# Where the ada sums are made, how rows are summed, and how wide the passes over the activations are

## The chip, the cores and the metric

The kernel runs on one core of one Trainium2 chip. Its time is the device time of one execution in microseconds (us), from the first instruction to the last; the number that counts is the median over runs. TensorE multiplies matrices, VectorE (DVE), ScalarE (ACT) and GpSimd (POOL) do the elementwise work, and SyncE (SP), ScalarE and GpSimd issue DMA transfers.

## The reference

Two blocks act on 256 tokens of width 1024, all in float32. The first has two layers, each a mixer (layer 0: pooling and a state space model; layer 1: two kinds of attention) and a gated feed-forward part, each followed by a layer norm over `ALPHA * x + h`:

```python
def swiglu(x, w_gate, w_up, w_down):
    return (jax.nn.silu(x @ w_gate) * (x @ w_up)) @ w_down      # D_FF = 2816
```

The second block takes a vector `c` and makes six rows of 1024 numbers from it, the ada rows (`m` = 0 to 5), which shift, scale and gate a short gated convolution and a squared-relu MLP:

```python
mod_lat = [m[:, None, :] for m in jnp.split(jax.nn.silu(c) @ ada_w[i] + ada_b[i], N_MOD, axis=-1)]
a_lat = modulate(rmsnorm(h_lat, g_pre), mod_lat[0], mod_lat[1])
y_lat = short_gated_conv(a_lat, sc_w_in[j], sc_conv[j], sc_w_out[j])
h_lat = h_lat + mod_lat[2] * rmsnorm(y_lat, g_post)
f_lat = squared_relu_mlp(modulate(rmsnorm(h_lat, g_pre_ff), mod_lat[3], mod_lat[4]), mlp_w_in[i], mlp_w_out[i])
h_lat = h_lat + mod_lat[5] * rmsnorm(f_lat, g_post_ff)
```

`ada_w` is 1024 x 6144, 24 MB, as much as the gate, up and down weights of 8 of the 11 feed-forward blocks.

## The kernel before

**Numbers in two parts.** Each weight chunk of 1 MB (128 partitions x 2048 float32) is loaded by SP into one of six slots, and is split there: ScalarE rounds it to fp32r (`hi`, L1136), VectorE subtracts (`lo`, L1575). Activations are split the same way into `x_hi` and `x_lo`. A product is then three fp32r passes of TensorE: hi with hi, hi with lo, lo with hi. In the projections (`col`, L565 to L567) the weight chunk's 128 columns are the stationary operand and 256 tokens stream past; in the products back to the model width (`tok3`, L572 to L574) the activations are stationary and 512 weight columns stream past. A slot is loaded again when its chunk has been used (`chunk_used`).

**A feed-forward part** (`ffn0` in layer 0, `ffn1` in layer 1) has 11 blocks of 256 hidden columns. In block i TensorE makes the gate and the up projection (a chunk each, 2 x 8 accumulation steps of three passes), into PSUM banks 4 and 5 or 6 and 7 by turns; then `rows_full` multiplies the hidden values of block i - 1 with their down chunk. ScalarE takes the silu of the gate out of PSUM (L1238), VectorE multiplies it with the up projection in PSUM (L1750, the hidden product), ScalarE and VectorE split the result (L1243, L1755). The last three down chunks (8, 9, 10) are left to the end, where each is multiplied for the first 128 tokens and then for the other 128, so that the layer norm of the first half can start early. Chunk 10 is split after block 10, with the first two chunks of the next stage: `split(first["odd"] + 1)` or `split(first["sc"] + 1)`. After that TensorE needs the normed, transposed rows before it can go on.

**The MLP** has 16 blocks of 256 hidden columns; the first three are made in halves, 13 go through `col`, relu on ScalarE (L1544) and a square on VectorE (L2112).

**The ada rows** are made during `ffn1`. GpSimd clears `modrow`, loads the bias, and loads 24 pieces of `ada_w` of 1 MB by turns into the two buffers `sq` and `r`; VectorE adds each piece, scaled by one number of silu(c) per partition, into `modrow` (`ada_step`, L423, 24 times, 2 or 3 in a block). What is left is a sum over the 128 partitions: `mod_sums` multiplies a row of `modrow` with a matrix of ones in float32 (L699), after blocks 4, 5, 7, 8 and 10, and the sixth in the convolution stage (`MOD_LAST`). ScalarE copies the sum back (`mod_copy`, L1217). When all 24 steps are done, GpSimd loads two rows of gains (`gain_row`, L482) over `sq`, and VectorE multiplies two ada rows with them (`gained`, L1723) at the end of its block 10, ahead of the split of down chunk 10 on the same queue:

```python
                    if name == "ffn1" and i == NF - 1:
                        gained(1, 0, 1.0)
                        gained(2, 1, 0.0)
```

Engines run their own queues in program order. The order of GpSimd's queue before, from layer 1's mixer on: rows of the next norm (`ln_rows("ln3")`), the clearing, the bias, the 24 pieces, a wait for all 24 steps, the two gain rows.

Of the kernel before, what the change touches and what calls it, by code (L numbers as in the profile page):

```python
# [11 lines left out]
P = 128  # L12
# [57 lines left out]
def build(nc, A, out):  # L70
    ctx = ExitStack()
    with ctx:
# [17 lines left out]
        x_hi = sb("x_hi", [P, KT, S], F32R)  # L90
        x_lo = sb("x_lo", [P, KT, S], F32R)
# [5 lines left out]
        ones = sb("ones", [P, P])  # L97
        d_skip = sb("d_skip_sb", [P, KT])
# [99 lines left out]
        def bank2(b):  # L198
            return PS[:, b, :].rearrange("p (a s) -> p a s", a=2)

# [212 lines left out]
        ADA_BLOCKS = range(1, 10)  # L413
        MOD_AT = {4: 0, 5: 1, 7: 2, 8: 3, 10: 4}
        MOD_LAST = 5
# [57 lines left out]
        def _(pool):  # L473
# [46 lines left out]

            pool.wait_ge(*sig_at("ln0", "x", 4))
            ln_rows("ln1")
            pool.wait_ge(*sig_at("ln1", "x", 4))
# [5 lines left out]
            pool.tensor_tensor(kr_cos[rr, :], kr[rr, 0, :], cos, ALU.mult).then_inc(sem("kr_cos"), 1)  # L529
            pool.wait_ge(*norm("kvn", "var", 1))  # L530
            for q in range(4):
                pool.wait_ge(sem("odd_evac"), 12 + q)
                pool.tensor_tensor(sq[rr, 2 * q:2 * q + 2, :], qm[rr, 2 * q:2 * q + 2, :],
                                   cos.rearrange("p (o s) -> p o s", o=1).to_broadcast([32, 2, S]), ALU.mult)\
                    .then_inc(sem("qm_cos"), 1)
# [3 lines left out]
                             .to_broadcast([32, MLA_H, S])).then_inc(sem("kr_rot"), 1)  # L539

            pool.wait_ge(*sig_at("ln2", "x", 4))
            ln_rows("ln3")
            pool.memset(modrow[:, :, :], 0.0).then_inc(sem("ada_zero"), 1)
            pool.wait_ge(sem("ada_zero"), 1)
            pool.dma_start(modrow[0:1, :, :].rearrange("p m d -> p (m d)"), A["ada_b_2"][0:1, :])\
                .then_inc(sem("ada_bias"), 16)
            for n in range(ADA_N):
                if n >= 2:
                    pool.wait_ge(sem("ada_fma"), n - 1)
                pool.dma_start(ada_raw[n % 2], A["ada_w_2"][0][n % KT * P:(n % KT + 1) * P, n // KT * CH:(n // KT + 1) * CH])\  # L550
                    .then_inc(sem(f"ada_landed{n % 2}"), 16)
# [8 lines left out]
        def _(pe):  # L560
# [15 lines left out]
            def col(c, bank, hi, lo, operand=None, between=None):  # L576
# [5 lines left out]
                for m in range(0, n, P):  # L582
# [3 lines left out]
                    for k in range(kt):  # L586
# [108 lines left out]
            def mod_sums(m, bank):  # L695

                pe.wait_ge(sem("ada_fma"), KT * (m // 2 + 1))
                for n in range(2):
                    last = pe.matmul(PS[:, bank + n, :], ones[:, :], modrow[:, m, n * HB:(n + 1) * HB], start=True, stop=True)  # L699
                last.then_inc(sem("mod_sum"), 1)  # L700

            def ffn(name, operand, after, src):
# [13 lines left out]
                for i in range(1, NF):  # L716
                    b = 6 - 2 * (i % 2)
                    pe.wait_ge(hid_done, o + i)
                    if name == "ffn1" and i - 1 in MOD_AT:
                        pe.wait_ge(sem("mod_row"), MOD_AT[i - 1] + 1)  # L720
                    col(at[name, "g", i], b, x_hi, x_lo)
# [3 lines left out]
                    col(at[name, "g", i] + 1, b + 1, x_hi, x_lo)  # L725
                    if name == "ffn1" and i in MOD_AT:
                        pe.wait_ge(hid_done, o + i + 1)
                        mod_sums(MOD_AT[i], 6 - 2 * ((i - 1) % 2))
# [164 lines left out]
            base = first["odd"]  # L893
            for h in range(2):
# [83 lines left out]
            def scores(a):  # L978
# [5 lines left out]
                if a == FOX_H:  # L984
                    pe.wait_ge(sem("odd_evac"), 19)
                    pe.wait_ge(sem("kr_rot"), 1)
# [54 lines left out]
            ffn("ffn1", "ln2", "pre", r_tok)  # L1041

# [20 lines left out]
            for q in range(1, 4):  # L1063
                for part in range(3):
                    col(at["sc", "c", q] + part, sc_bank(3 * q + part), x_hi, x_lo)
                    if q == 1 and part == 0:
# [4 lines left out]
                        mod_sums(MOD_LAST, 0)  # L1071
                if q == 1:
                    pe.wait_ge(sem("mod_row"), MOD_LAST + 1)
# [31 lines left out]
            for i in range(3, NM):  # L1105
                pe.wait_ge(sem("mlp_relu"), i - 3 + 4)
# [1034 lines left out]
```

## Time and profile before

| | |
|---|---|
| median of three runs | 980.95 us (979.12 to 981.13) |
| the profiled execution | 980.15 us, of which the span from first to last instruction is 978.3 us |
| TensorE busy | 944.3 us of the span, granted clock 0.997 |
| VectorE, ScalarE, GpSimd busy | 645.9, 466.6 and 62.0 us |
| weights split (L1575 on VectorE, L1136 on ScalarE) | 336.1 and 278.1 us |
| DMA | 190.5 MB, 195 GB/s in the mean |

A busy engine is not the same as one that sets the end. Matmul records overlap (each lasts longer than the distance to the next), so what a matmul costs in a dense stretch is the distance between the starts, not its duration.

### The profile page before, as it was taken

Reading aid. Unit: us, or ns where it says so; the run is one execution under the profiler, and the core shown is the slowest. Engines: PE = TensorE matmul, PEld = TensorE weight load, DVE = VectorE, ACT = ScalarE, POOL = GpSimd, SP = SyncE. Lnnn points to the kernel's source line nnn. Section 1 sums busy time; section 2 is a strip of 40 time slices with the busy share of each in tenths; the row PEclk is TensorE's granted clock in tenths of the full one; section 3 lists DMA queues with packets and bytes.
Section 4 is the critical chain, followed back from the end, with each engine's and each line's share of the span. In section 5 each row is a group of like instructions: output and inputs, shape, how many; then the busy total and the mean of one; then the engine's idle time right before and its main releaser. Section 6 shows DMA issues by size and latency. Waiting matters only on the chain.

```text
span 978.3 us, 15123 instructions
## 1 busy us (share of the span) xinstructions
PE 944.3 (97%) x6537; PEld 862.8 (88%) x6537; DVE 645.9 (66%) x737; ACT 466.6 (48%) x577; POOL 62.0 (6%) x79
## 2 busy tenths in 40 slices
PE   6999989999999999999899999999899999999997
PEld 6999879999999799876699989998799989999986
DVE  4976896645454863676659788788866865555554
ACT  6556744434343465755544343445344644444442
POOL 2034000000000000220030001000000000000000
PEclk9999999999999999999999999999999999999999
DMA  9744466565565453412579999995566456566531
GB/s 280 239 131 130 136 205 219 186 195 178 181 203 177 130 173 110 133 44 87 176 283 331 381 317 338 308 348 165 185 198 198 130 175 213 175 194 191 174 128 44
DMA packets 122282, 190.52 MB, mean 195 GB/s; under 512 B 6566, under 2 KB 103080, under 8 KB 119144
## 3 DMA queue, kind: packets, MB, share of 16 engines
q1 hardware_dynamic: 115184, 156.94, 49.5%
q0 software_dynamic: 5616, 31.78, 8.8%
q8 instruction: 52, 0.85, 0.3%
q10 hardware_dynamic: 1416, 0.83, 0.3%
q14 instruction: 14, 0.11, 0.0%
HBM read 188.49 MB, written 1.05 MB: 194 GB/s over the span
## 4 chain that ended last, share of the span: by engine, by line
PE 80%; DVE 10%; ACT 5%; issue 3%; DMA 1%; DVEq 0%; POOL 0%; ACTq 0%
PE PS L565 15%; PE PS L567 15%; PE PS L566 15%; PE PS L572 10%; PE PS L574 9%; PE PS L573 9%; DVE lo L1575 3%; ACT hi L1136 2%; PE PS L699 1%; PE PS L663 1%; DMA raw<-even_w_in 1%; DVE r L1645 1%; ACT hid L1437 1%; DMA sq<-norm_gains 1%; ACT sq L1321 1%
## 5 line engine op out<-in xcount | busy, mean ns | idle before, releaser
L1575 DVE TENSOR_TENSOR lo<-raw,hi 128x2048 fp32r<-128x2048 f32 (+2 forms) x150 | 336.1, 2258 | 168.8 <-ACT hi L1136 168.6
L565 PE MATMUL PS<-x_hi,hi 128*128 128x256 f32 x1320 | 374.4, 284 | 1.9 <-DVE x_lo L1772 1.9
L567 PE MATMUL PS<-x_hi,lo 128*128 128x256 f32 x1320 | 372.3, 282 | 0.0
L566 PE MATMUL PS<-x_lo,hi 128*128 128x256 f32 x1320 | 371.7, 282 | 0.0
L1136 ACT ACTIVATE hi<-raw 128x2048 fp32r<-128x2048 f32 (+2 forms) x150 | 278.1, 1880 | 10.2 <-DMA raw<-even_w_in 8.0
L565 PEld LDWEIGHTS PS<-x_hi,hi 128*128 128x128 f32 x1320 | 251.2, 190 | 4.3 <-DVE lo L1575 2.3
L566 PEld LDWEIGHTS PS<-x_lo,hi 128*128 128x128 f32 x1320 | 251.2, 190 | 1.9 <-issue 0.5
L567 PEld LDWEIGHTS PS<-x_hi,lo 128*128 128x128 f32 x1320 | 251.2, 190 | 0.0
L572 PE MATMUL PS<-hi,hid_hi 128*128 128x512 f32 x352 | 141.2, 401 | 1.1 <-DVE lo L1575 0.7
L574 PE MATMUL PS<-hi,hid_lo 128*128 128x512 f32 x352 | 138.6, 394 | 0.0
L573 PE MATMUL PS<-lo,hid_hi 128*128 128x512 f32 x352 | 138.5, 393 | 0.0
L572 PE MATMUL PS<-hi,x_hi 128*128 128x256 f32 (+1 forms) x256 | 81.7, 319 | 7.7 <-DVE x_lo L1674 3.5
L572 PEld LDWEIGHTS PS<-hi,hid_hi 128*128 128x128 f32 x352 | 66.1, 188 | 17.5 <-issue 3.7
L574 PEld LDWEIGHTS PS<-hi,hid_lo 128*128 128x128 f32 x352 | 66.0, 188 | 15.6
L574 PE MATMUL PS<-hi,x_lo 128*128 128x256 f32 (+1 forms) x256 | 79.8, 312 | 0.0
L573 PE MATMUL PS<-lo,x_hi 128*128 128x256 f32 (+1 forms) x256 | 79.6, 311 | 0.0
L573 PEld LDWEIGHTS PS<-lo,hid_hi 128*128 128x128 f32 x352 | 66.0, 188 | 15.1 <-issue 1.2
L1238 ACT ACTIVATE gate_s<-PS 128x512 f32<-128x512 f32 x20 | 12.0, 599 | 103.2 <-PE PS L567 103.2
L572 PEld LDWEIGHTS PS<-hi,x_hi 128*128 128x128 f32 x256 | 48.8, 191 | 13.3 <-issue 8.1
L574 PEld LDWEIGHTS PS<-hi,x_lo 128*128 128x128 f32 x256 | 48.8, 191 | 2.8
L1243 ACT ACTIVATE hid_hi<-hid 128x512 fp32r<-128x512 f32 x20 | 12.6, 632 | 80.9 <-DVE hid L1750 80.9
L573 PEld LDWEIGHTS PS<-lo,x_hi 128*128 128x128 f32 x256 | 49.0, 191 | 2.5
(280 smaller groups left out, 825.5 us busy)
## 6 DMA issues: line engine op xcount, KB each, us to landing
raw<-ffn_w_gate SPq DMA_DIRECT2D x22, 1024.0 KB, 5.4
raw<-ffn_w_up SPq DMA_DIRECT2D x22, 1024.0 KB, 5.5
raw<-ffn_w_down SPq DMA_DIRECT2D x22, 1024.0 KB, 5.0
raw<-mlp_w_in SPq DMA_DIRECT2D x16, 1024.0 KB, 5.6
raw<-mlp_w_out SPq DMA_DIRECT2D x16, 1024.0 KB, 5.0
sq<-ada_w POOLq DMA_DIRECT2D x12, 1024.0 KB, 6.3
r<-ada_w POOLq DMA_DIRECT2D x12, 1024.0 KB, 7.2
raw<-sc_w_in SPq DMA_DIRECT2D x12, 1024.0 KB, 5.3
```

Of the source, the lines that this page charges most:

```text
L565: pe.matmul(dst, wh, hi, start=start, stop=False, skip_group_check=True)
L566: pe.matmul(dst, wh, lo, start=False, stop=False, skip_group_check=True)
L567: return pe.matmul(dst, wl, hi, start=False, stop=stop_, skip_group_check=True)
L572: pe.matmul(dst, hi, wh, start=start, stop=False, skip_group_check=True)
L573: pe.matmul(dst, hi, wl, start=False, stop=False, skip_group_check=True)
L574: return pe.matmul(dst, lo, wh, start=False, stop=stop_, skip_group_check=True)
L663: last = pe.transpose(PS[:, 2 * h + n, j * P:(j + 1) * P], src[:, h, o:o + P], ident)
L699: last = pe.matmul(PS[:, bank + n, :], ones[:, :], modrow[:, m, n * HB:(n + 1) * HB], start=True, stop=True)
L1136: act.activation(split_view("hi", c), split_view("raw", c), ACT.Copy).then_inc(hi_split, 1)
L1238: act.activation(gate_s[:, i % 2, :, :], bank2(6 - 2 * (i % 2)), ACT.Silu).then_inc(silu, 1)
L1243: act.activation(hid_hi[:, i % 3, :, :], hid[:, i % 2, :, :], ACT.Copy).then_inc(hi_done, 1)
L1575: dve.tensor_tensor(split_view("lo", c), split_view("raw", c), split_view("hi", c).bitcast(F32), ALU.subtract)\
```

## The change

1. **Two thirds of the ada sums move into `ffn0`.** 16 of the 24 pieces and steps (rows 0 to 3) are done in `ffn0`, two in each of blocks 1 to 8, and 8 (rows 4 and 5) in `ffn1`, one in each of blocks 1 to 8. The rows are summed after blocks 6, 7, 9 and 10 of `ffn0` and after 9 and 10 of `ffn1`. Since the attention stage uses the memory of `modrow`, rows 0 to 3 are stored in device memory (`mods`) and loaded back at the start of `ffn1`.
2. **Row sums in two fp32r parts.** `mod_high` (ScalarE) and `mod_low` (VectorE) split a row into `mod_part`, and `mod_sums` is four fp32r matmuls. `mod_part` takes the memory of `lnrow`, the rows of the next norm, so `ln_rows("ln1")` and `ln_rows("ln3")` are now loaded after the fourth and the sixth sum. The two gain rows stand behind `ln_rows("ln3")`.
3. **512-column passes.** `x_hi` and `x_lo` become one tensor `x_both`. `wide_cols` replaces `col` in blocks 1 to 10 of both feed-forward parts and in 13 blocks of the MLP. The hi part of the weights meets both parts of x in one pass of 512 columns, the lo part meets `x_hi` in one of 256. The products hi-hi and hi-lo land side by side in PSUM, so that each chunk fills two banks (gate 4 and 5, up 6 and 7, no turns). ScalarE copies the second half out (`low_part`), VectorE adds the first; silu and relu come after the sum.

```diff
-        lnrow = sb("lnrow", [P, 2, D])
+        with ExitStack() as row_views:
+            lnrow = sb("lnrow", [P, 2, D], F32, row_views)
+        mod_part = sb("mod_part", [P, 2, D], F32R)
...
-        ADA_BLOCKS = range(1, 10)
-        MOD_AT = {4: 0, 5: 1, 7: 2, 8: 3, 10: 4}
-        MOD_LAST = 5
+        ADA_STEPS = {"ffn0": (0, 2 * KT), "ffn1": (2 * KT, ADA_N)}
+        MOD_AT = {"ffn0": {6: 0, 7: 1, 9: 2, 10: 3}, "ffn1": {9: 4, 10: 5}}
...
@@ GpSimd
             pool.wait_ge(*sig_at("ln0", "x", 4))
+            ada_loads(0, 4)
+            pool.wait_ge(sem("mod_sum"), 4)
             ln_rows("ln1")
+            pool.wait_ge(sem("mod_row"), 4)
+            pool.dma_start(mods[0:1, :], modrow[0:1, 0:4, :].rearrange("p m d -> p (m d)")).then_inc(sem("mods_moved"), 16)
...
             pool.wait_ge(*sig_at("ln2", "x", 4))
+            ada_loads(4, 6)
+            pool.wait_ge(sem("mod_sum"), 6)
             ln_rows("ln3")
...
             pool.wait_ge(sem("ada_fma"), ADA_N)
             gain_row(0)
             gain_row(1)
...
@@ TensorE
+            def wide_cols(c, bank, between=None):
+
+                pe.wait_ge(lo_split, c + 1)
+                for m in range(2):
+                    if between and m:
+                        between()
+                    cols = slice(m * P, (m + 1) * P)
+                    for k in range(KT):
+                        wh, wl = slot("hi", c)[:, k, cols], slot("lo", c)[:, k, cols]
+                        pe.matmul(PS[:, bank + m, :], wh, x_both[:, :, k, :], start=k == 0, stop=False, skip_group_check=True)
+                        last = pe.matmul(PS[:, bank + m, 0:S], wl, x_hi[:, k, :], start=False, stop=k == KT - 1,
+                                         skip_group_check=True)
+                last.then_inc(chunk_used, 1)
...
                 for n in range(2):
-                    last = pe.matmul(PS[:, bank + n, :], ones[:, :], modrow[:, m, n * HB:(n + 1) * HB], start=True, stop=True)
+                    for part in range(2):
+                        last = pe.matmul(PS[:, bank + n, :], ones_r[:, :], mod_part[:, part, n * HB:(n + 1) * HB],
+                                         start=part == 0, stop=part == 1, skip_group_check=True)
...
@@ ScalarE, block i
                     split(g + 2)
+                    split(g + 3)
+                    if i in MOD_AT[name]:
+                        mod_high(MOD_AT[name][i])
+                    n = (NF - 1) * (name == "ffn1") + i
                     act.wait_ge(chunk_used, g + 1)
                     if i >= 2:
                         act.wait_ge(hid_done, o + i)
-                    act.activation(gate_s[:, i % 2, :, :], bank2(6 - 2 * (i % 2)), ACT.Silu).then_inc(silu, 1)
-                    split(g + 3)
+                    act.activation(gate_s[:, i % 2, :, :], PS[:, 4:6, S:2 * S], ACT.Copy).then_inc(sem("low_part"), 1)
+                    act.wait_ge(sem("gate_sum"), n)
+                    act.activation(gate_s[:, i % 2, :, :], gate_s[:, i % 2, :, :], ACT.Silu).then_inc(silu, 1)
+                    act.wait_ge(chunk_used, g + 2)
+                    act.activation(b_sb[:, i % 2, :, :], PS[:, 6:8, S:2 * S], ACT.Copy).then_inc(sem("low_part"), 1)
...
@@ VectorE, block i
+                        if i in MOD_AT[name]:
+                            mod_low(MOD_AT[name][i])
+                        n = (NF - 1) * (name == "ffn1") + i
+                        dve.wait_ge(sem("low_part"), 2 * n - 1)
+                        dve.tensor_tensor(gate_s[:, i % 2, :, :], PS[:, 4:6, 0:S], gate_s[:, i % 2, :, :], ALU.add)\
+                           .then_inc(sem("gate_sum"), 1)
+                        dve.wait_ge(sem("low_part"), 2 * n)
+                        link(dve.tensor_tensor(hid[:, i % 2, :, :], PS[:, 6:8, 0:S], b_sb[:, i % 2, :, :], ALU.add))
                         dve.wait_ge(silu, o + i + 2)
-                        dve.wait_ge(chunk_used, g + 2)
-                        dve.tensor_tensor(hid[:, i % 2, :, :], gate_s[:, i % 2, :, :], bank2(7 - 2 * (i % 2)), ALU.mult)\
+                        dve.tensor_tensor(hid[:, i % 2, :, :], gate_s[:, i % 2, :, :], hid[:, i % 2, :, :], ALU.mult)\
                            .then_inc(hid_done, 1)
...
@@ MLP: TensorE, ScalarE, VectorE
-                col(at["mlp", "m", i], 4 + i % 3, x_hi, x_lo, between=opening_turns if i == 3 else None)
+                wide_cols(at["mlp", "m", i], 6 - 2 * (i % 2), between=opening_turns if i == 3 else None)
...
-                act.activation(relu_s[:, i % 3, :, :], bank2(4 + i % 3), ACT.Relu).then_inc(sem("mlp_relu"), 1)
+                b = 6 - 2 * (i % 2)
+                act.activation(relu_s[:, i % 3, :, :], PS[:, b:b + 2, S:2 * S], ACT.Copy).then_inc(sem("low_part"), 1)
...
+                dve.tensor_tensor(relu_s[:, i % 3, :, :], PS[:, b:b + 2, 0:S], relu_s[:, i % 3, :, :], ALU.add)\
+                   .then_inc(sem("mlp_relu"), 1)
```

`ada_loads(m0, m1)` is the clearing, the bias and the pieces of before for a range of rows, with the reload of `mods` in the second call.

## Rows read from the trace of the kernel before

**Rows 1.** Chain of waits that ended last: shares of the span by engine.

```profile
PE 80%; DVE 10%; ACT 5%; issue 3%; DMA 1%; DVEq 0%; POOL 0%; ACTq 0%
```

**Rows 2.** Two stretches: us, busy PE, PEld, DVE, ACT, POOL, clock, DMA share, GB/s.

```profile
165.00:318.00 153.00, 153.00 (x1106) 144.64 (x1105) 76.29 (x47) 62.57 (x48) 0.00 (x0) 1.00 0.59 186
505.00:657.00 152.00, 152.00 (x1056) 139.39 (x1055) 119.20 (x66) 61.93 (x48) 11.65 (x22) 1.00 0.95 341
```

**Rows 3.** TensorE in order of time, ffn0 block 3: start, duration, line.

```profile
199.73 0.28 PE L565 MATMUL PS<-x_hi,hi 128*128 128x256 f32 x1
...
204.41 0.39 PE L572 MATMUL PS<-hi,hid_hi 128*128 128x512 f32 x1
...
206.97 0.40 PE L574 MATMUL PS<-hi,hid_lo 128*128 128x512 f32 x1
```

**Rows 4.** The same view in ffn0 block 2.

```profile
176.07 0.28 PE L565 MATMUL PS<-x_hi,hi 128*128 128x256 f32 x1
...
187.42 0.40 PE L572 MATMUL PS<-hi,hid_hi 128*128 128x512 f32 x1
...
192.67 0.40 PE L574 MATMUL PS<-hi,hid_lo 128*128 128x512 f32 x1
```

**Rows 5.** Groups of instructions by line: busy us, mean ns, idle before.

```profile
L1575 DVE TENSOR_TENSOR lo<-raw,hi 128x2048 fp32r<-128x2048 f32 x145 | 329.3, 2289 | 155.1 <-ACT hi L1136 154.8
L423 DVE SCALAR_TENSOR_TENSOR modrow<-sq,silu_c,modrow 128x2048 f32<-128x2048 f32 x12 | 28.1, 2345 | 0.0
L699 PE MATMUL PS<-modrow,ones 128*128 128x512 f32 x24 | 11.3, 592 | 0.0
L1238 ACT ACTIVATE gate_s<-PS 128x512 f32<-128x512 f32 x20 | 12.0, 599 | 103.2 <-PE PS L567 103.2
L1217 ACT ACTIVATE modrow<-PS 128x1024 f32<-128x1024 f32 x6 | 6.2, 1030 | 1.5 <-PE PS L699 1.5
```

**Rows 6.** Chain of waits in order of time: two row sums on it.

```profile
564.92 1.72 PE PS L699 x4
...
717.84 1.72 PE PS L699 x4
```

**Rows 7.** Chain of waits in order of time, end of ffn0.

```profile
318.02 0.70 DVE hid L1750
318.74 0.63 ACT hid_hi L1243
319.37 1.82 ACT hi L1136
321.21 6.70 DVE lo L1575 x3
327.91 1.19 DVE r L1645 x2
```

**Rows 8.** VectorE in order of time: the hidden product of ffn1's block 10.

```profile
668.34 0.69 DVE L1750 TENSOR_TENSOR hid<-gate_s,PS 128x512 f32<-128x512 f32 x1 [1.10 <-PE PS L567]
```

**Rows 9.** Chain of waits in order of time, end of ffn1.

```profile
665.13 0.52 POOL sq L482
665.65 5.46 DMA sq<-norm_gains
...
672.35 1.22 DVE modrow L1723
673.57 4.03 DVE lo L1575 x2
...
680.17 1.20 DVE r L1645 x2
```

**Rows 10.** DMA issues by tile: count, KB each, median us to landing.

```profile
r<-ada_w POOLq DMA_DIRECT2D x12, 1024.0 KB, 7.2
```

**Rows 11.** As rows 2: two short stretches before ffn0.

```profile
125.50:132.20 6.70, 3.42 (x18) 2.78 (x17) 6.46 (x7) 5.56 (x6) 0.00 (x0) 1.00 0.86 273
133.50:136.90 3.40, 3.40 (x10) 2.63 (x9) 3.30 (x4) 0.00 (x0) 0.00 (x0) 0.50 0.00 0
```

More of the change, by code:

```diff
@@ L716, in ffn @@
                 for i in range(1, NF):
[L717 to L721, printed above, removed]
+                    if i == 1:
+                        pe.wait_ge(hid_done, o + 1)
+                    else:
+                        pe.wait_ge(sem("ffn_silu"), o + i + 1)
+                    if i - 1 in MOD_AT[name]:
+                        pe.wait_ge(sem("mod_row"), MOD_AT[name][i - 1] + 1)
+                    wide_cols(at[name, "g", i], 4)
                     if i == 1:
@@ L724, in ffn @@
                         turn_hidden(0, hid[:, 0, :, :]).then_inc(sem("hidden_turned"), 1)
-                    col(at[name, "g", i] + 1, b + 1, x_hi, x_lo)
-                    if name == "ffn1" and i in MOD_AT:
+                    if i > 1:
                         pe.wait_ge(hid_done, o + i + 1)
-                        mod_sums(MOD_AT[i], 6 - 2 * ((i - 1) % 2))
+                    wide_cols(at[name, "g", i] + 1, 6)
+                    if i in MOD_AT[name]:
+                        pe.wait_ge(sem("ffn_silu"), o + i + 2)
+                        mod_sums(MOD_AT[name][i], 4)
                     if i <= NF - TAIL:
@@ L1243, in ffn @@
                     act.activation(hid_hi[:, i % 3, :, :], hid[:, i % 2, :, :], ACT.Copy).then_inc(hi_done, 1)
-                    if name == "ffn1" and i in MOD_AT:
-                        mod_copy(MOD_AT[i], 6 - 2 * ((i - 1) % 2))
+                    if i in MOD_AT[name]:
+                        mod_copy(MOD_AT[name][i], 4)
                     if i < NF - 1:
@@ L1504, in _ @@
                 if q == 1:
-                    mod_copy(MOD_LAST, 0)
                     sc_hi(0)
@@ L1724, in gained, with mod_low @@
                                          op0=ALU.add, op1=ALU.mult).then_inc(sem("gained"), 1)
+            def mod_low(m):
+                dve.wait_ge(sem("mod_high"), m + 1)
+                dve.tensor_tensor(mod_part[:, 1, :], modrow[:, m, :], mod_part[:, 0, :].bitcast(F32), ALU.subtract)\
+                   .then_inc(sem("mod_low"), 1)
             def ffn(name):
@@ L1731, in ffn @@
                     g = at[name, "g", i]
-                    ada = list(range(ADA_N * (i - 1) // 9, ADA_N * i // 9)) if name == "ffn1" and i in ADA_BLOCKS else []
-                    if ada and i == 1:
-                        dve.wait_ge(sem("silu_c_ready"), 1)
-                        dve.wait_ge(sem("ada_bias"), 16)
+                    n0, n1 = ADA_STEPS[name]
+                    ada = list(range(n0 + (n1 - n0) * (i - 1) // 8, n0 + (n1 - n0) * i // 8)) if 1 <= i <= 8 else []
+                    if i == 1:
+                        dve.wait_ge(sem("a_silu_c"), 2)
+                        dve.wait_ge(sem("ada_bias"), 16 + 16 * (name == "ffn1"))
                     split(g + 2)
-                    if len(ada) > 2:
-                        ada_step(dve, ada.pop(0))
                     if i == 0:
```

97 lines of the change are left out of this document (60 added, 37 removed).

## The prediction

> **What bounds the kernel now.** The chain of waits comes first: 80% of the span lies on TensorE, 10% on VectorE and 5% on ScalarE [rows 1]. So TensorE's own time counts nearly everywhere, and the rest of the end lies in the few places where TensorE waits for the others. The busy times by stretch show where it does not wait: in the blocks of ffn0 and of ffn1 it is busy for 153.0 of 153.0 us and 152.0 of 152.0 us at full clock, while VectorE works 76 and 119 us, and in ffn1 DMA moves 341 GB/s at a share of 0.95 [rows 2]. Even with 2 or 3 ada steps in a block and DMA almost full, ffn1 costs TensorE nothing but its row sums. What moves out of VectorE or DMA in ffn1's blocks therefore brings nothing by itself; what shortens TensorE's stream brings its full length.
>
> The length of that stream is read from start to start, not from durations. In block 3 of ffn0 there are 39 passes of 256 columns from 199.73 to 204.41, so 120.0 ns each, and 11 steps between 512-column passes from 204.41 to 206.97, so 232.7 ns each [rows 3]. Block 2, with chunks in other slots, is a little quicker: 96 passes from 176.07 to 187.42 are 118.2 ns each, and 23 steps from 187.42 to 192.67 are 228.3 ns [rows 4].
>
> **The wide passes.** A step of the accumulation was three passes of 256 columns, 3 x 120.0 = 360.0 ns. It becomes one of 512 and one of 256, 232.7 + 120.0 = 352.7 ns; in the quicker slots 354.6 becomes 346.5. I take 7 ns a step. There are 16 steps in a chunk, 20 chunks in each feed-forward part and 13 in the MLP: 640 + 208 = 848 steps, **5.9 us saved**. No row has these two passes in turn, so this is a bound question. From below: if what a pass costs beyond its columns went with the columns and not with the pass, 768 columns would cost 3 x 120.0 as now, nothing saved. From above: the quicker slots' passes everywhere in the new form against the slower ones in the old, 360.0 - 346.5 = 13.5 ns, 11.4 us. The middle value stands nearest to the rows, which have both widths in the same block.
>
> The Trainium skill (TensorE: Matmul & The Clock Gate, section on the back-to-back issue gap) gives a gap of the columns over 2.4 GHz plus about 2.5 ns for any width. By it a step would go from 327.6 to 325.0 ns and the 848 steps would save an estimated 2.2 us, and the sum below would come out 3.7 us higher. This case's trace does not agree with that: 120.0 and 232.7 ns are 13 and 19 ns above the columns [rows 3], so a pass fewer is worth more than the page has it.
>
> Around these passes ScalarE and VectorE get work: per feed-forward block two copies of 0.60 us [rows 5] on ScalarE, and two additions of some 0.69 us on VectorE. In the middle of a part nothing waits for it. TensorE's block is 32 x 0.353 + 24 x 0.233 = 16.9 us. VectorE's, in ffn0, is three splits at 2.29, two ada steps at 2.35 [rows 5], four operations of 0.7 and, in blocks 6 and 7, a `mod_low` of some 1.2: 14.4 to 15.6 us. It keeps at least 1.3 us of room. The single pair of banks for the gate is free again when the silu of the block before is done, and the up projection and the down product, 11.2 us, lie between. DMA in ffn0 needs 5 chunks, 5.24 MB, in 16.9 us, 310 GB/s, less than the 341 that ffn1 had without a wait [rows 2]. These edits cost nothing there. The MLP's blocks have no ada steps and more room still.
>
> **The row sums.** Each cost TensorE 1.72 us in the chain [rows 6], because the float32 passes run in two: 24 for 12 products, 1.72 us for four of them. In fp32r it is four passes of 512 columns, 0.93 us. Before, five of the six lay in TensorE's stream (four in ffn1, one in the convolution stage); the one after block 10 of ffn1 is not in the chain, since the chain runs over GpSimd and VectorE there. After, four lie in the stream (blocks 6, 7, 9 of ffn0, 9 of ffn1). 5 x 1.72 - 4 x 0.93 = **4.9 us saved**. The splitting of the rows, about 1.0 us on ScalarE (as the copy L1217 [rows 5]) and 1.2 on VectorE, hides behind gate i.
>
> **The end of ffn0.** Here the chain leaves TensorE: hidden product 318.02, its hi part, the split of down chunk 10 on ScalarE, three splits on VectorE, and the norm's first sum at 327.91 [rows 7]. All of it is in program order, so whatever is put ahead delays the norm and with it TensorE's restart. In front of the product come a copy of 0.60 and an addition of 0.70; between hi part and split comes `mod_copy` of 1.03, which ran nowhere in ffn0 before. 0.60 + 0.70 + 1.03 = **2.3 us lost**. The fourth row sum costs TensorE 0.93 us in the same place, within that time. `ln_rows("ln1")` is issued a microsecond after the product and is needed some 14 later; it lands in time. Bounds: 1.3 if the copy of the row finds a gap, 3.0 if a signal is lost at each of the added steps.
>
> **The end of ffn1.** Here is the part of the change that costs most. Before, the hidden product of block 10 started at 668.34 [rows 8]; the gain rows were issued at 665.13, three microseconds ahead of it, and `gained` could start at 672.35 - 1.22 = 671.13, 2.8 us after the product [rows 9]. Now the gain rows stand on GpSimd's queue behind `ln_rows("ln3")`, and this behind the sixth row sum, which ends about 0.9 us after block 10. Four transfers of 512 KB are issued from then on, 0.52 us each. The nearest row for 2 MB on this queue is the second of two ada pieces, 7.2 us to landing [rows 10], 7.7 after the first one's issue. So `gained` starts at 0.9 + 7.7 + 0.2 = 8.8 us, **6.0 us later** than before. Behind it on VectorE wait the splits of down chunk 10 and of the next stage's first two chunks, then the norm [rows 9]; TensorE has the passes of chunks 8 and 9 for the first half (24 x 0.233 = 5.6 us) and then nothing. The copy and the addition ahead of the product are hidden in this wait, and so is `mod_copy`. Bounds: the gain pair alone took 0.52 + 5.46 us, with the two issues ahead 7.0, so 5.1 us later; if four transfers took twice the pair's 6.0, 10.1 later.
>
> TensorE then idles from 0.9 + 5.6 = 6.5 to 8.8 + 2.4 + 2.2 = 13.4 us, 7 us on end. Before ffn0, after a stretch in which it was busy for only 3.42 of 6.70 us, 3.4 us ran at a granted clock of 0.50, the lower of its two levels, 1.2 GHz [rows 11]. I expect the same here. 3.4 us at half clock are 1.7 us of lost work; 48 passes (11.2 us) still stand before the restart, beside VectorE's splits and norm, which are as long. I take **1.2 us**, between 0 (all in the shadow of VectorE) and 3.4 (the slow stretch twice as long).
>
> **The sum.** -5.9 - 4.9 + 2.3 + 6.0 + 1.2 = -1.3 us on the profiled execution's 980.15: 978.85. The median of the runs is 0.8 above that execution, so 979.7. 0.2% of the time, 2.0 us, is about what a measurement of this kernel can tell from no change; the forecast is no change.
>
> **The rivals.** (a) The wait for the gain rows does not reach the restart, because VectorE's splits were late for TensorE anyway, or the rows land as early as before: without 6.0 and 1.2, 972.5. Against it: the chain of before already runs over this very transfer [rows 9]. (b) The new passes stream at the upper bound: 5.5 us less, 974.2. For it: the distances differ by slot [rows 4], so something besides columns sets them. (c) On the other side: the passes save nothing, a cost by columns, 979.7 + 5.9 = 985.6. That decides as soon as the pair is dearer than 358 ns. The rule of the Trainium skill (TensorE: Matmul & The Clock Gate, back-to-back issue gap) lies between, at an estimated 983.4. (d) Slower too: ffn0 becomes bound by the ada pieces. VectorE's queue then stops at an ada step, and behind it wait hid_lo and the split of the next up chunk. It decides once DMA gives less than 310 GB/s; at 300 a block takes 17.5 us, 8 blocks 4.8 us more, 984.5. Against it: 341 GB/s in ffn1 [rows 2].
>
> **The chances.** Forecast 0.60, with a range of its own from 977 to 983 (faster 0.13, same 0.39, slower 0.08); (a) 0.12 and (b) 0.11, faster; (c) 0.10, of which 0.01 is same; (d) 0.07, slower. Faster 0.36, same 0.40, slower 0.24. The range that leaves out about 2 in 10 goes from (a) to (c): 972.0 to 985.5.
>
> **What would show it.** Distances of 350 to 354 ns from one 512-column pass of `wide_cols` to the next; the row sums' passes at 0.23 us; TensorE busy all through ffn0's blocks; at the end of ffn0 12.2 us from the copy to the norm's first sum; at the end of ffn1 about 7 us of idle TensorE in front of down chunk 10, released by VectorE, whose own wait is for the DMA of the gain rows, then a stretch at the lower clock. The prediction is wrong if that wait is under 4 us, if a step is under 345 or over 357 ns, or if TensorE waits for a silu or a split inside ffn0.

## The result and the profile after

The changed kernel takes 992.1 us in the median (990.0 to 992.3, 4 runs), the kernel before 980.95 (979.1 to 981.1, 4 runs): 1.011 times as long (1.0095 to 1.0125). It is slower by 11 us where 1.3 us less was forecast, and lies outside the range. The profiled execution took 990.04 us; its span is 988.3 us, 10.0 more than that of before.

By stage, from the start of one landmark on TensorE to the start of the same one in both traces, the difference is made of these parts (the stages not listed make -0.2 us together):

| stretch | before, us | after, us | difference |
|---|---|---|---|
| ffn0, blocks 1 to 10 | 159.2 | 162.0 | +2.8 |
| end of ffn0, to the transposes | 15.25 | 17.44 | +2.2 |
| ffn1, blocks 1 to 10 | 166.1 | 163.8 | -2.3 |
| end of ffn1, to the transposes | 20.12 | 31.31 | +11.2 |
| convolution stage | 99.08 | 97.22 | -1.9 |
| MLP, to the last instruction | 191.0 | 189.2 | -1.8 |

What TensorE waited for, in the view of waits (total us, times, longest):

```profile
PE PS L589 <- DVE lo L1629: 16.0, 4, 11.2
PE PS L787 <- DMA x_tok<-x: 6.7, 1, 6.7
PE PS L623 <- issue: 5.6, 2, 2.8
```

The second line is the loading of x at the start. The first is the wait for the gain rows, 11.2 us in its longest piece. The third had no counterpart: TensorE stood still twice for 2.8 us ahead of a wide projection (L623). "issue" means that no releaser was recorded, so it has to be looked for by hand. The place is the start of block 10. TensorE in order of time there, in ffn0:

```profile
305.24 1.11 PE L731 MATMUL PS<-mod_part,ones_r 128*128 128x512 f32 x4
309.17 0.47 PE L623 MATMUL PS<-x_both,hi 128*128 128x512 f32 x1 [2.82 <-issue]
```

And ScalarE over the same time:

```profile
305.44 0.60 ACT L1292 ACTIVATE small<-PS 128x512 f32<-128x512 f32 x1 [0.38 <-PE PS L624]
307.53 0.63 ACT L1296 ACTIVATE hid_hi<-hid 128x512 fp32r<-128x512 f32 x1 [1.49 <-DVE hid L1819]
308.06 1.00 ACT L1263 ACTIVATE modrow<-PS 128x1024 f32<-128x1024 f32 x1
```

The row sum (L731) of block 9 goes into banks 4 and 5, the gate's. They are free when `mod_copy` (L1263) has emptied them, and that copy stands on ScalarE behind `hid_hi`, which waits for the hidden product on VectorE: it ends at 309.06, and the gate of block 10 starts at 309.17. After the other blocks' sums `rows_full` comes first, 5.5 us of down product, and covers the copy. Behind block 9 there is none, because chunks 8, 9 and 10 are left to the end.

The chain of waits from there to the end of ffn1, where the same thing happened:

```profile
652.88 0.93 PE PS L731 x4
653.81 2.83 issue
656.64 0.76 PE PS L623
657.62 0.43 PE PS L623
...
670.71 0.94 PE PS L731 x4
671.65 0.28 issue
671.93 1.04 POOL lnrow L482 x2
672.98 0.51 POOL sq L486
673.49 10.10 DMA sq<-norm_gains
683.75 1.08 issue
684.84 1.22 DVE modrow L1780
686.05 2.21 DVE lo L1629
688.40 0.77 PE PS L589
689.17 0.43 PE PS L590
689.60 0.43 PE PS L591
```

Against [rows 9] three things stand out. The wait ahead of block 10 is there again. The transfers of the end are the predicted ones in the predicted order, but the last gain row lands at 683.6, 11.7 us after the first of the four issues, where 7.7 was forecast. And after either wait the passes of 512 columns take 0.43 us in place of 0.23: the lower clock. The stretches (clock is the third figure from the end):

```profile
656.60:660.00 3.40, 3.36 (x11) 2.91 (x12) 1.63 (x1) 3.40 (x2) 0.00 (x0) 0.50 0.21 69
660.00:664.00 4.00, 4.00 (x18) 3.44 (x18) 4.00 (x3) 1.08 (x2) 0.00 (x0) 0.68 0.00 0
664.00:668.00 4.00, 4.00 (x26) 3.48 (x24) 0.69 (x2) 1.23 (x2) 0.00 (x0) 1.00 0.42 116
...
672.00:678.00 6.00, 5.24 (x23) 3.88 (x21) 1.45 (x3) 5.17 (x5) 2.02 (x4) 1.00 1.03 295
```

In block 10 of ffn1 TensorE ran at 1.2 GHz until about 662.6, and the 64 passes took 219 ns each in the mean against 176 in block 10 of ffn0, after an equal wait: 63 x 43 ns = 2.7 us. The last row has the four transfers of the end in it; the DMA engines are full there, at a share of 1.03.

### The profile page after: what moved, and what is told of

Its sections match the earlier page's. It is cut to its first block, busy times and chain, and to the rows that moved or that the text cites. A ratio compares the mean times of both kernels' runs of the same rounds, so it can differ in the third digit from the quotient of the medians.

```text
span 988.3 us, 13563 instructions
## 1 busy us (share of the span) xinstructions
PE 936.5 (95%) x5689; PEld 821.9 (83%) x5689; DVE 685.5 (69%) x797; ACT 496.5 (50%) x623; POOL 64.3 (7%) x83
## 4 chain that ended last, share of the span: by engine, by line
PE 72%; DVE 6%; ACT 3%; issue 3%; DMA 1%; POOL 0%; DVEq 0%
PE PS L623 20%; PE PS L624 10%; PE PS L589 10%; PE PS L590 9%; PE PS L591 9%; PE PS L582 3%; PE PS L583 3%; PE PS L584 3%; DVE lo L1629 2%; ACT hi L1175 1%; DMA sq<-norm_gains 1%; PE PS L694 1%; ACT hid L1490 1%; DVE gate_s L2055 1%; DVE stats L1706 0%
## 5 line engine op out<-in xcount | busy, mean ns | idle before, releaser
L623 PE MATMUL PS<-x_both,hi 128*128 128x512 f32 x848 | 300.5, 397 | 5.6 <-issue 5.6
L624 PE MATMUL PS<-x_both,lo 128*128 128x256 f32 x848 | 238.7, 282 | 0.0
L623 PEld LDWEIGHTS PS<-x_both,hi 128*128 128x128 f32 x848 | 160.5, 189 | 43.2 <-issue 6.5
L624 PEld LDWEIGHTS PS<-x_both,lo 128*128 128x128 f32 x848 | 161.2, 190 | 1.3
L582 PE MATMUL PS<-x_both,hi 128*128 128x256 f32 (+1 forms) x472 | 134.9, 286 | 1.2 <-DVE x_both L1842 1.1
L583 PE MATMUL PS<-x_both,hi 128*128 128x256 f32 (+1 forms) x472 | 133.2, 282 | 0.0
L584 PE MATMUL PS<-x_both,lo 128*128 128x256 f32 (+1 forms) x472 | 133.2, 282 | 0.0
L582 PEld LDWEIGHTS PS<-x_both,hi 128*128 128x128 f32 (+1 forms) x472 | 89.9, 191 | 2.2 <-DVE lo L1629 1.4
L583 PEld LDWEIGHTS PS<-x_both,hi 128*128 128x128 f32 (+1 forms) x472 | 90.0, 191 | 0.4 <-issue 0.2
L584 PEld LDWEIGHTS PS<-x_both,lo 128*128 128x128 f32 (+1 forms) x472 | 89.9, 191 | 0.0
L589 PE MATMUL PS<-hi,x_both 128*128 128x256 f32 (+1 forms) x256 | 81.1, 317 | 7.6 <-DVE x_both L1728 3.4
L591 PE MATMUL PS<-hi,x_both 128*128 128x256 f32 (+1 forms) x256 | 79.1, 309 | 0.0
L590 PE MATMUL PS<-lo,x_both 128*128 128x256 f32 (+1 forms) x256 | 79.1, 309 | 0.0
```

The costliest lines, as they stand in the source:

```text
L582: pe.matmul(dst, wh, hi, start=start, stop=False, skip_group_check=True)
L583: pe.matmul(dst, wh, lo, start=False, stop=False, skip_group_check=True)
L584: return pe.matmul(dst, wl, hi, start=False, stop=stop_, skip_group_check=True)
L589: pe.matmul(dst, hi, wh, start=start, stop=False, skip_group_check=True)
L590: pe.matmul(dst, hi, wl, start=False, stop=False, skip_group_check=True)
L591: return pe.matmul(dst, lo, wh, start=False, stop=stop_, skip_group_check=True)
```

## The experiments

The kernel before ran beside each: beside `copy_first` it took 980.1 us in the median, and beside the other ten kernels, in three groups, 981.0, 981.6 and 981.0. Each one is the kernel after with the edit shown, where nothing else is said, and ratios are to the kernel before. For the kernel after they stand against 1.011.

**What the waits of block 9 are made of.** In block 9 the copy of the row sum is put ahead of `hid_hi`, right behind the copy of the up projection:

```diff
+                    if i == NF - 2:
+                        mod_copy(MOD_AT[name][i], 4)
                     act.wait_ge(hid_done, o + i + 2)
...
-                    if i in MOD_AT[name]:
+                    if i in MOD_AT[name] and i != NF - 2:
                         mod_copy(MOD_AT[name][i], 4)
```

> One edit to the kernel after (992.1 us): in block 9 of both feed-forward parts ScalarE takes the row sum out of the gate's banks straight after the copy of the up projection's low half, not after the hi part of the hidden product. In the kernel after the sum's passes end near 306.8 us, ScalarE is idle for 1.49 us ahead of hid_hi, and the copy starts at 308.06, so TensorE waits from the last pass to 309.16. My theory: what TensorE waits for in block 9 is this copy; it then starts some 1.2 us earlier, the gap of 3.0 us ahead of block 10 falls to about 1.8 in each part, and if block 10 of the second part then runs at the full clock, 2.4 us more come back: 989.7 us, or 987.3 with the clock. Rival: TensorE waits for the silu or the hidden product of block 9 as well (both end by 307.5), the gap stays 3 us, and the time stays 992 us.

Measured: 986.38 us (983.45 to 987.86, 6 runs), ratio 1.0053 (1.0032 to 1.0073), so 5.7 us less than the kernel after from an edit that only reorders two instructions of one engine. TensorE and ScalarE in its trace, at the same place:

```profile
307.78 1.11 PE L731 MATMUL PS<-mod_part,ones_r 128*128 128x512 f32 x4
310.05 0.47 PE L623 MATMUL PS<-x_both,hi 128*128 128x512 f32 x1 [1.16 <-issue]
```

```profile
308.93 1.02 ACT L1263 ACTIVATE modrow<-PS 128x1024 f32<-128x1024 f32 x1 [0.34 <-PE PS L731]
310.07 0.63 ACT L1298 ACTIVATE hid_hi<-hid 128x512 fp32r<-128x512 f32 x1
```

Both waits shrink from 2.8 to 1.16 us, 3.3 us together, and block 10 of ffn1 runs at the full clock (176 ns a pass), 2.7 us. Together that is 6.0; the measured 5.7 is known to about 2.5 us, since it compares two groups. The copy, 1.02 us, now starts right behind the sum and fills what is left of the wait. My theory stands, the rival (the silu or the product holds TensorE) falls. Whether the half clock went because the wait was 1.7 us shorter is not shown by these two waits: ffn0 of the kernel after had the longer wait without it.

The other way to lose this wait is to have no row sum behind block 9:

```diff
-        MOD_AT = {"ffn0": {6: 0, 7: 1, 9: 2, 10: 3}, "ffn1": {9: 4, 10: 5}}
+        MOD_AT = {"ffn0": {5: 0, 6: 1, 8: 2, 10: 3}, "ffn1": {8: 4, 10: 5}}
...
-                    ada = list(range(n0 + (n1 - n0) * (i - 1) // 8, n0 + (n1 - n0) * i // 8)) if 1 <= i <= 8 else []
+                    ada = list(range(n0 + (n1 - n0) * (i - 1) // 7, n0 + (n1 - n0) * i // 7)) if 1 <= i <= 7 else []
```

> The ada steps are spread over blocks 1 to 7 and not 1 to 8, so that the rows can be summed after blocks 5, 6, 8 and 10 of ffn0 and 8 and 10 of ffn1, and never after block 9, which has no down product behind it. If the two waits of 3.0 us for the copy of a summed row (before the gate projection of block 10) come from that place, both go, and with the second the half-clock stretch in block 10 of ffn1 (2.4 us): 8.4 us less than the changed kernel, 983.7. Rival: two or three ada steps a block with a row sum fill VectorE's queue, and new waits inside ffn0 take the place of these; then the time stays at 990 to 994.

Measured: 988.65 us (986.72 to 989.95, 4 runs), ratio 1.0066 (1.0049 to 1.0083). It lies between the two figures expected. Both waits of block 9 and the half clock of block 10 are gone, but 5.3 us of waits came back in a new place:

```profile
PE PS L731 <- ACT gate_s L1290: 5.3, 4, 2.4
```

The steps fall as 2, 2, 2, 3, 2, 2, 3. Blocks 4 and 7, right before those with a sum, have three, so VectorE is late with the gate's addition, ScalarE with the silu, and the sum's banks are free late. The sum is moved out of one wait into another. Behind the longest, 2.4 us, stands again a stretch of 3.4 us at 1.2 GHz (from 242.0).

**The gain rows.** They are issued ahead of the rows of the norm and of the wait for the sixth sum:

```diff
             ada_loads(4, 6)
-            pool.wait_ge(sem("mod_sum"), 6)
-            ln_rows("ln3")
             pool.wait_ge(sem("ada_fma"), ADA_N)
             gain_row(0)
             gain_row(1)
+            pool.wait_ge(sem("mod_sum"), 6)
+            ln_rows("ln3")
```

> The two gain rows are asked for as soon as the 24 ada steps are done, ahead of the wait for the sixth row sum and ahead of the rows of the third norm. Nothing else changes. If the 11.3 us for which TensorE waits in front of the last down chunk of ffn1 come from where the gain rows stand on GpSimd's queue, they have landed before block 10 ends; that wait falls to about 1.5 us, as at the end of ffn0, the half-clock stretch behind it goes too, and the stretch from the sixth row sum to the next transposes falls from 31.3 to about 20.7 us: 981.5 us in all, 10.6 less than the changed kernel. Rival: the queue of splits on VectorE behind a longer product chain is what makes TensorE wait, and the transfer only hides it; then the wait falls by no more than half and the time by 5 us at most, to 987.

Measured: 982.14 us (979.17 to 983.9, 10 runs), ratio 1.0005 (0.999 to 1.0019). That is 10 us back, as expected within 1 us. The end of ffn1, 31.31 us in the kernel after, takes 20.5. In the chain VectorE goes from the product to the gain rows with no transfer between:

```profile
676.10 0.64 ACT hid_hi L1296
...
677.37 2.35 DVE modrow L1780 x2
679.73 4.04 DVE lo L1629 x2
```

In between lies the order that waits for the sixth sum but not for the norm's rows: `gain_row(0)`, `gain_row(1)`, then `ln_rows("ln3")`, all behind the sum.

> The changed kernel with the gain rows asked for after the sixth row sum, but ahead of the two rows of the third norm. If the landing took 11.7 us after the first issue because four transfers of 512 KB share the queue, the gain rows land 6 to 7 us after their issue, the wait in front of down chunk 10 falls from 11.3 to 6 or 7 us, and the time by 4.5 to 5 us, to 987.3. Rival: the weight transfers beside them make any transfer slow at this place, then the gain rows still need 9 us or more and the time falls by 1 to 2 us, the two issues ahead.

Measured: 989.38 us (988.81 to 992.26, 4 runs), ratio 1.0088 (1.0066 to 1.0109), 2.7 us less than the kernel after. The pair was issued at 674.08 and landed at 683.1, 9.0 us later. So the rival was nearer: of the 11.7 us, 2.7 go with the two transfers ahead. That share is rough, since the same four transfers took between 10.4 us (`sums_fp32`) and 12.1 (`copy_first`) in the traces. In the kernel before, the pair took 6.0 [rows 9], issued 3.2 us ahead of the hidden product of block 10. The 3 us between are not explained by order. They may be the norm's rows and the weight loads in flight with them, which I did not separate. Full DMA engines alone do not explain them: from 664.0 to 671.5 the kernel before had a DMA share of 1.02 at 343 GB/s, and `gains_between` 0.78 at 258 GB/s from 672 to 684.

**The width of the passes.** Here everything stays as after (both parts of a chunk in its two banks, copies and additions), but a step is three passes of 256 columns again:

```diff
-                        pe.matmul(PS[:, bank + m, :], wh, x_both[:, :, k, :], start=k == 0, stop=False, skip_group_check=True)
-                        last = pe.matmul(PS[:, bank + m, 0:S], wl, x_hi[:, k, :], start=False, stop=k == KT - 1,
+                        pe.matmul(PS[:, bank + m, 0:S], wh, x_hi[:, k, :], start=k == 0, stop=False, skip_group_check=True)
+                        pe.matmul(PS[:, bank + m, 0:S], wl, x_hi[:, k, :], start=False, stop=k == KT - 1,
+                                  skip_group_check=True)
+                    for k in range(KT):
+                        wh = slot("hi", c)[:, k, cols]
+                        last = pe.matmul(PS[:, bank + m, S:2 * S], wh, x_lo[:, k, :], start=k == 0, stop=k == KT - 1,
```

> Each step of the wide projections is three passes of 256 columns again (hi with hi, lo with hi, then hi with lo into the other half of the bank); copies, additions, banks and everything else stay as in the changed kernel. If the width alone saves 7 ns a step, as the prediction took it, this costs 848 x 7 = 5.9 us: 998.0. The traces of both kernels side by side give 8 to 9 ns a step in ffn0, so up to 8 us. Rival: the cost goes with the columns, then the time stays at 992 within 1 us.

Measured: 997.43 us (995.47 to 997.71, 4 runs), ratio 1.0158 (1.0141 to 1.0175). The width is worth 5.3 us, 6.3 ns for each of the 848 steps, against 7 ns forecast; the interval leaves some 2 us either way. The traces give more: in the feed-forward blocks a step takes 353 to 360 ns here and 346 to 353 in the kernel after, 7 to 9 ns less. The two profiled executions hide part of that, because this one lost 1.2 us less to the lower clock in block 10 of ffn1.

**The row sums' number format.** `mod_sums` multiplies the float32 row again, as before, and all the rest stays, `mod_high` and `mod_low` too:

```diff
-                    for part in range(2):
-                        last = pe.matmul(PS[:, bank + n, :], ones_r[:, :], mod_part[:, part, n * HB:(n + 1) * HB],
-                                         start=part == 0, stop=part == 1, skip_group_check=True)
+                    last = pe.matmul(PS[:, bank + n, :], ones[:, :], modrow[:, m, n * HB:(n + 1) * HB], start=True, stop=True)
```

> The changed kernel with the row sums as two float32 products again; the splitting of the rows is still made, though nothing reads it. Each sum then costs TensorE 1.72 us and not 0.93. Five of the six stand where TensorE or a queue behind it sets the end (blocks 6, 7 and 9 of ffn0, 9 of ffn1, and the sixth, behind which the gain rows wait): 5 x 0.79 = 4.0 us more, 996.1. Rival: the two sums in block 9 run beside ScalarE's and VectorE's work on the hidden values, for which the copy waits anyway, so that only three count: 994.5.

Measured: 992.03 us (991.29 to 993.19, 4 runs), ratio 1.011 (1.0092 to 1.0128), no difference to the kernel after. Both expected figures were too high. In the trace a sum takes 1.72 us again, which is 0.79 more. It adds to TensorE's stream behind blocks 6 and 7, 1.6 us. Behind block 9 it takes its time from the wait for the copy (2.04 us of idle time in place of 2.83), and at the end of ffn0 it is hidden (17.45 us from the sum to the transposes, as before the edit). The sixth sum does put off the row transfers by 0.8 us, but in this execution they landed 10.4 us after the first issue and not 11.7. So the equal times can be in part chance, and the interval leaves room for 2 us.

**Both repairs together**, `gains_first` and `sums_early`:

> Both edits together. They are in different places, so their gains should add: 10.6 + 8.4 = 19.0 us less than the changed kernel, 973.1, which would be 0.8% faster than the kernel before. If they overlap (a shared half-clock stretch, or a wait that moves from one place to the other), less than 16 us.

Measured: 981.68 us (977.2 to 985.95, 10 runs), ratio 0.9998 (0.9976 to 1.0019). Of the 8.6 us by which the expected 973.1 was missed, the trace has 5.7 as waits for the silu at the sums' new places and some 1.7 as a stretch of 3.4 us at 1.2 GHz behind the longest of them (from 243.0).

So the steps of ffn0 were set by hand, in a kernel that is `both` otherwise:

```diff
+                    ends = [n0, 3, 6, 8, 10, 12, 14, 16] if name == "ffn0" else [n0 + (n1 - n0) * j // 7 for j in range(8)]
+                    ada = list(range(ends[i - 1], ends[i])) if 1 <= i <= 7 else []
```

> Gain rows first and no sum after block 9, as in the run with both edits, but the 16 ada steps of ffn0 lie 3, 3, 2, 2, 2, 2, 2 on blocks 1 to 7, so that no block with three steps stands before one with a row sum. In the run with both edits TensorE waited 2.6 and 2.5 us for the silu of the gate in front of the sums after blocks 5 and 8, each behind a block with three ada steps. If VectorE's queue was late there by one ada step (2.35 us), both waits go and 5 us with them: 976.5. Rival: seven blocks are too few for 16 steps wherever the third ones lie; then the waits only move, 981 to 982.

Measured: 977.92 us (977.01 to 981.95, 7 runs), ratio 0.9972 (0.9957 to 0.9987). The waits at the sums after blocks 5 and 8 are gone, and two others, 0.8 and 3.8 us, stand in blocks 2 and 3. Its chain of waits there:

```profile
192.65 2.36 DVE modrow L427
195.00 0.28 issue
195.29 8.09 DMA r<-ada_w
...
203.40 2.35 DVE modrow L427
205.75 2.22 DVE lo L1629
...
208.10 0.77 PE PS L589
208.87 0.43 PE PS L590
```

A stretch of 3.4 us at 1.2 GHz lies behind the second. Two buffers take two pieces ahead. The third step of a block waits for a piece that is loaded only once the buffer is free, and behind it on VectorE waits a split that TensorE needs. In block 10 of both parts of the next kernel ScalarE also splits down chunk 10 ahead of `mod_copy`:

```diff
+                    if i == NF - 1:
+                        split(g + 4)
                     if i in MOD_AT[name]:
                         mod_copy(MOD_AT[name][i], 4)
```

> The same, and in block 10 ScalarE splits down chunk 10 before it copies the summed row out. That takes 1.0 us out of the chain at the end of ffn0, whose length the prediction put at 0.60 + 0.70 + 1.03 more than before. Expected: 11.2 us from TensorE's last row sum of ffn0 to the norm's first sum where it was 12.3, and 1 us less than the run before it in this call. At the end of ffn1 the gains on VectorE stand ahead of the split anyway, nothing there. Rival: the splits on VectorE are the chain, then nothing in either place.

Measured: 977.6 us (976.85 to 980.42, 7 runs), ratio 0.996 (0.9948 to 0.9972). The end of ffn0 got 0.4 us shorter (17.1 to 16.7 us from the sum to the transposes), not 1.0, since `mod_copy` now delays the split behind it. The times of the two runs do not tell them apart.

Then the three-step blocks are set apart, with `ends = [n0, 2, 4, 7, 9, 11, 14, 16]` and the rest as in `spread_copy_late`:

> This is the version before it (spread_copy_late, 977.6 us) with the sixteen ada steps of the first feed-forward part as 2, 2, 3, 2, 2, 3, 2 over blocks 1 to 7 in place of 3, 3, 2, 2, 2, 2, 2. In spread two waits of TensorE for VectorE's lo, 1.1 and 4.1 us, stood around blocks 2 and 3, behind an ada piece that landed 8.1 us after the one before. My theory: two blocks of three steps in a row outrun the two ada buffers; set apart, with lighter blocks before them, they don't, both waits go, and with the stretch at half clock behind them the run gives 977.6 - 5 = about 972.6 us (971.5 to 974.5). Rival: any block with three steps waits for its third piece, since only two are loaded ahead; then one wait of 3 to 4 us stands in block 3 and one in block 6, and the time is 977 to 980 us.

Measured: 974.9 us (974.44 to 975.68, 5 runs), ratio 0.9943 (0.993 to 0.9957). That is 2.7 us less than the version before it where 5 were expected, and above the range given. Its longest wait for a split is 1.9 us, and at the sums it has little:

```profile
PE PS L589 <- DVE lo L1631: 4.5, 4, 1.9
...
PE PS L731 <- ACT gate_s L1290: 1.3, 3, 0.6
```

A part of the rival is true, since block 3 still has a transfer of 5.14 us on its chain and TensorE waits 0.6 us at the sum of block 5, but the large waits are gone. This version is the fastest, 0.6% ahead of the kernel before.

**The move alone.** The last question is what moving two thirds of the ada sums is for. This kernel is `gains_first` with all steps and sums in ffn1, three steps a block, and so without the store and reload of rows 0 to 3:

```diff
-        ADA_STEPS = {"ffn0": (0, 2 * KT), "ffn1": (2 * KT, ADA_N)}
-        MOD_AT = {"ffn0": {6: 0, 7: 1, 9: 2, 10: 3}, "ffn1": {9: 4, 10: 5}}
+        ADA_STEPS = {"ffn0": (0, 0), "ffn1": (0, ADA_N)}
+        MOD_AT = {"ffn0": {}, "ffn1": {4: 0, 5: 1, 7: 2, 8: 3, 9: 4, 10: 5}}
```

> This is gains_first (982.1 us) with all twenty-four ada steps back in the second feed-forward part, three a block over blocks 1 to 8, and all six row sums there (after blocks 4, 5, 7, 8, 9 and 10), as in the kernel before; the six rows need no store and reload then. The wide passes, the fp32r row sums and the early gain rows stay. My theory: TensorE does the same work in either order, the move brings nothing by itself, and VectorE, which has three steps to add in a block besides the splits that the projections need, still ends inside the 17.4 us of a block: 982.1 less the 3 us wait of block 9 of the first part, which has no row sum now, so 978 to 981 us. The end of the first part gets 2.2 us shorter too, as its transposes have no last row to wait for, so 977.5 us as the one number. Rival: without two thirds of the steps moved away, VectorE or the third ada piece of each block falls behind the shorter blocks, TensorE waits 1 us or more in each of blocks 1 to 8 of the second part, and the time is 985 us or more; then the move was what gave the wide passes room.

Measured: 996.35 us (995.63 to 998.92, 4 runs), ratio 1.0164 (1.0149 to 1.0179). The rival's time is right: 14 us slower than `gains_first`. TensorE waits, though not in every block as the rival had it. 5.3 and 3.5 us stand at the sums after blocks 4 and 7, and stretches of 3.4 us at 1.2 GHz begin with the end of both (from 572.3 and 630.3). Two stretches of ffn1:

```profile
PE PS L727 <- ACT gate_s L1285: 10.6, 3, 5.3
PE PS L585 <- DVE lo L1623: 8.5, 6, 1.9
```

```profile
520.00:540.00 20.00, 19.29 (x102) 16.21 (x101) 18.30 (x12) 10.00 (x10) 1.66 (x4) 1.00 0.92 324
540.00:560.00 20.00, 18.66 (x100) 15.80 (x99) 17.80 (x12) 9.49 (x9) 2.04 (x4) 1.00 0.96 348
```

VectorE is busy for 18.30 and 17.80 of 20 us, at a DMA share of 0.92 and 0.96. The chain runs over ada steps, the splits behind them and ada pieces of 5 to 6 us in turn. But a busy VectorE is not yet a late one. The kernel before had this in the first of the two stretches, with no wait of TensorE:

```profile
520.00:540.00 20.00, 20.00 (x146) 18.90 (x146) 18.92 (x11) 7.22 (x6) 1.90 (x4) 1.00 1.00 364
```

Two things differ from it besides the wide passes and the additions. The kernel before put its 24 steps into nine blocks (`ADA_BLOCKS = range(1, 10)`), two in each of blocks 1, 4 and 7, and `one_part` puts three into each of eight; and each sum now needs a `mod_low`. An estimate from the durations in the traces: three splits at 2.29, three steps at 2.35, four operations of 0.7 and a `mod_low` of 1.2 are 17.9 us of VectorE in a block with a sum, where TensorE needs 17.6 in the kernel after (block 6 of ffn0); with two steps they are 15.6. So three steps leave such a block no room, and what comes late stays late from block to block. One block of the kind is carried (block 6 of `spread36` has three steps and a sum, and no wait). Whether ffn1 could hold all 24 steps in nine blocks, as before, no run shows.

## Why the prediction was wrong, point by point

**The step that failed** is the sentence on the gate's banks: "The single pair of banks for the gate is free again when the silu of the block before is done, and the up projection and the down product, 11.2 us, lie between", with its verdict "These edits cost nothing there". It holds for blocks 1 to 8. Two things were left out. The row sum uses the same pair of banks after the silu, so they are free when `mod_copy` is done, not the silu. And block 9, behind which the change puts a sum in either part, has no down product behind it. From the sum's last pass to the next gate that is 3.0 us more, twice, 6.0 us, and 2.7 us of half clock behind the second. `copy_first` shows the cause of the waits: the copy.

**The second step is a term that was sized wrongly**, the landing of the gain rows. The mechanism, its place and those who wait behind it were as predicted. But "the nearest row for 2 MB on this queue" gave 7.7 us for the four transfers, and they took 11.7, 4.0 more. The upper bound named for it, 10.1 later than before, was right: the whole end of ffn1 is 11.2 us longer, with the half clock, where 7.2 were forecast. 979.7 + 6.0 + 2.7 + 4.0 = 992.4, by the median 992.1. That it comes out so closely is partly luck, since a stretch at half clock came behind only one of the two equal waits. `gains_first` shows that this stall, once removed, gives 10 us back.

**Wide passes**, -5.9: right, 5.3 by `narrow` and 7 to 9 ns a step by the traces. Steps of 346 to 353 ns show in the trace; here 31 steps from 294.15 to 304.89 are 346.5 ns each, as computed for the quicker slots:

```profile
294.15 0.39 PE L623 MATMUL PS<-x_both,hi 128*128 128x512 f32 x1
...
304.89 0.40 PE L623 MATMUL PS<-x_both,hi 128*128 128x512 f32 x1
```

The estimate by the Trainium skill (TensorE: Matmul & The Clock Gate, section on the back-to-back issue gap) was 2.2 us for the same edit. That section gives the formula for a matmul by itself and says that in a stream of weight loads and matmuls both set the spacing, so it did not have to hold here. The measurement decides against the figure.

**Row sums**, -4.9: right in the count, not in the reason. A sum takes 0.93 us in the stream (the chain above), and ffn1 and the convolution stage lose 6.0 and 1.7 us of sums while ffn0 gains 2.8. Of the 4.9, one sum fewer in the stream is 1.7 and the format of the other four 3.2. `sums_fp32` finds at most some 2 us of these 3.2 and its trace 1.6, because in block 9 a longer sum only takes from the wait that the change itself made.

**The end of ffn0**, +2.3: right, 2.2. **Half clock** at the end of ffn1, +1.2: right, mechanism and size. From the end of the two gain products on VectorE to the transposes it is 14.6 us in the kernel before and in `gains_first`, both at full clock there, and 15.8 in the kernel after.

**The rivals.** (a), a hidden gain wait, is false in the kernel after and is what `gains_first` builds. (b) and (c) are false by `narrow`. (d) is false as it was put, since ffn0's blocks 1 to 9 are dense with two steps each, but its mechanism is real: with three steps in a block (`spread`) the piece is late, the split behind the ada step too, and TensorE waits.

**Not settled:** why the pair of gain rows takes 9.0 us when it goes first at that point and 6.0 in the kernel before, and what of the 14 us of `one_part` is the wide passes and what the packing of three steps into a block.

## What to carry to other kernels

When a bank gets a second user, ask at every place where it is used what lies between that use and the next, and above all at the first and last turns of a loop, where the covering work is missing. Transfers put behind others on a queue have to be priced from their own kind in the same surroundings, and a load that needs nothing from the wait ahead of it belongs ahead of that wait. When a faster inner loop adds work to another engine, add up that engine's work block by block, the fullest ones too: here two ada steps a block left VectorE room, and three in every block left none.

## What was not expected of the hardware

A wait of TensorE of 2.8 us was followed by a stretch at 1.2 GHz in ffn1 and by none in ffn0 of the same execution (block 10 at 219 and 176 ns a pass). In the profiles of `gains_first` and `gains_between`, with the same two waits, block 10 took 200 and 203, and 203 and 203 ns a pass. `narrow`, with the same waits too, had the stretch in ffn1 and none in ffn0. So six of these eight waits had such a stretch behind them. Of eight waits between 2.0 and 2.6 us in the feed-forward parts of `sums_fp32`, `sums_early`, `both`, `spread_copy_late` and `one_part`, four had one. With the wait cut to 1.16 us neither block had one, and where no wait stood there (`sums_early`, `both`, `spread`) they took 174 to 175 ns. A short wait in a dense stretch thus cost 1.5 to 2.7 us more in block 10 where the stretch came, which was not every time, and its price can only be given as a range.

The four row transfers, 2 MB in all as they land, took 10.4 to 12.1 us from the first issue to the last landing (`sums_fp32` 10.4, `sums_early` 10.9, kernel after 11.7, `narrow` 11.8, `copy_first` 12.1), where two ada pieces of 1 MB each took 7.7.
